# Sixteen pieces of dense work in an attention loop: one at a time in two of three steps, not two at a time in every third

## The reference

```python
def trunk_layer(x, cond, p, layer_idx, ctx):
    mod = jax.nn.silu(cond) @ p['w_ada'] + p['b_ada']            # six shifts, scales, gates
    sh1, sc1, g1, sh2, sc2, g2 = split(mod, 6)
    h = rmsnorm(x, p['g_pre_mix']) * (1 + sc1) + sh1
    y, new_ctx = token_mixer(h, p, layer_idx, ctx)
    x = x + g1 * rmsnorm(y, p['g_post_mix'])
    h = rmsnorm(x, p['g_pre_ffn']) * (1 + sc2) + sh2
    x = x + g2 * rmsnorm(expert_choice_ffn(h, ...), p['g_post_ffn'])

def token_mixer(h, p, layer_idx, ctx):
    q, k, v, z, xbc, dt_raw, g = split(h @ p['w_in'])
    ...
    g_attn, g_ssd = split(sigmoid(g), 2)
    merged = g_attn * (o_attn @ p['w_o_attn']) + g_ssd * (o_ssd @ p['w_o_ssd'])
    return merged @ p['w_out'], new_ctx

def diff_attention(q, k, v, lam, lam_init, w_subln):             # per block of 128 queries, 8 heads
    s = einsum('bqhmd,bkhmd->bhmqk', q, k) * scale               # two score maps per head
    pr = softmax(s)
    a = pr[:, :, 0] - lam * pr[:, :, 1]
    o = einsum('bhqk,bkhe->bqhe', a, v)
    return rmsnorm(o, w_subln) * (1.0 - lam_init)
```

## Time and profile before

| | us |
|---|---|
| median of 3 runs | 1917.01 (1915.61 to 1917.22) |
| the profiled execution | 1913.68 |
| its span, first to last instruction | 1911.9 |
| up to the attention stage | 634.0 |
| attention stage (634.0 to 800.3) | 166.3 |
| projections and routing (800.3 to 954.0) | 153.7 |
| experts (954.0 to the end) | 957.9 |

### The profile page before, as it was taken

The page is one execution under the profiler, slowest core; times in us unless marked ns, Lnnn a source line. Parts: engine busy times, 40 slices in busy tenths (PEclk is TensorE's granted clock), DMA queues, the critical chain, the costliest instruction groups (busy, mean ns, idle before and its releaser), DMA issues.

```text
span 1911.9 us, 22583 instructions
## 1 busy us (share of the span) xinstructions
PE 1587.8 (83%) x9263; PEld 934.3 (49%) x9263; DVE 521.7 (27%) x1450; ACT 257.8 (13%) x607; POOL 90.2 (5%) x118
## 2 busy tenths in 40 slices
PE   6998888989999876798798777977779777787775
PEld 4654544545565443455464444544435444454442
DVE  2439779750021245524600001000010000100002
ACT  1323222210010112102100000000001000100001
POOL 0002212210000000100000000000000000000000
PEclk9998998989999888898799999999999999999998
DMA  7233333312323114644099999999999999999993
GB/s 321 89 135 121 110 132 110 143 45 88 110 101 129 56 44 191 239 175 178 0 380 426 426 428 426 426 427 428 427 422 427 427 428 427 421 428 427 427 427 156
DMA packets 40305, 512.92 MB, mean 268 GB/s; under 512 B 4608, under 2 KB 4736, under 8 KB 10384
## 3 DMA queue, kind: packets, MB, share of 16 engines
q1 hardware_dynamic: 33696, 488.32, 61.6%
q0 software_dynamic: 6368, 22.58, 3.2%
q10 hardware_dynamic: 144, 0.59, 0.1%
HBM read 506.65 MB, written 4.82 MB: 268 GB/s over the span
## 4 chain that ended last, share of the span: by engine, by line
PE 49%; DMA 34%; DVE 12%; issue 3%; ACT 1%; POOL 1%; SPq 0%; DVEq 0%; ACTq 0%
DMA arena<-in_expert_chunks 33%; PE psum L356 14%; PE psum L779 13%; PE psum L367 9%; PE psum L568 4%; DVE arena L1394 1%; PE psum L380 1%; DVE arena L1383 1%; PE psum L798 1%; DVE arena L1466 1%; PE psum L543 1%; PE psum L404 1%; PE psum L414 1%; PE psum L553 1%; PE psum L652 0%
## 5 line engine op out<-in xcount | busy, mean ns | idle before, releaser
L779 PE MATMUL psum<-arena 128*64 128x256 f32 x6144 | 708.3, 386 | 165.2 <-DMA arena<-in_expert_chunks 136.3
L779 PEld LDWEIGHTS psum<-arena 128*64 128x64 f32 x6144 | 432.5, 138 | 431.5 <-DMA arena<-in_expert_chunks 190.3
L356 PE MATMUL psum<-arena 128*128 128x384 f32 x1024 | 352.0, 503 | 11.0 <-ACT arena L1088 7.7
L356 PEld LDWEIGHTS psum<-arena 128*128 128x128 f32 x1024 | 200.8, 198 | 149.8 <-issue 21.2
L1665 DVE TENSOR_TENSOR arena<-arena,psum 128x256 f32<-128x256 f32 x64 | 26.9, 421 | 774.1 <-ACT arena L1143 774.1
L367 PE MATMUL psum<-arena 128*128 128x512 f32 x384 | 166.4, 592 | 1.8 <-DVE arena L1514 1.8
L367 PEld LDWEIGHTS psum<-arena 128*128 128x128 f32 x384 | 72.4, 190 | 90.2 <-issue 87.5
L1143 ACT ACTIVATE arena<-psum 128x256 f32<-128x256 f32 x64 | 24.6, 384 | 616.0 <-PE psum L779 616.0
L568 PE MATMUL psum<-arena 128*128 128x384 f32 x256 | 84.8, 494 | 1.8 <-DVE arena L1355 1.2
L1150 ACT ACTIVATE arena<-psum 32x256 f32<-32x256 f32 x128 | 48.0, 375 | 272.8 <-PE psum L779 271.7
L856 POOL TENSOR_TENSOR arena<-arena 128x1 f32<-128x1 f32 x45 | 25.8, 575 | 1200.4 <-DVE arena L1539 941.4
(11 more groups left out here) (236 smaller groups left out, 990.5 us busy)
## 6 DMA issues: line engine op xcount, KB each, us to landing
arena<-in_expert_chunks SPq DMA_DIRECT2D x192, 2048.0 KB, 25.5
arena<-in_mixer_chunks SPq DMA_DIRECT2D x40, 2048.0 KB, 8.0
arena<-cs_rows POOLq DMA_DIRECT2D x24, 512.0 KB, 5.7
arena<-in_h_cm POOLq DMA_DIRECT2D x8, 256.0 KB, 3.0
out_state<-arena POOLq DMA_DIRECT2D x8, 256.0 KB, 3.4
arena<-in_x_cm SPq DMA_DIRECT2D x1, 1536.0 KB, 8.7
arena<-in_x_sample POOLq DMA_DIRECT2D x1, 1024.0 KB, 5.8
out_xs<-arena POOLq DMA_DIRECT2D x2, 512.0 KB, 2.9
```

Source lines behind the costliest of these rows:

```text
L356: mm = pe.matmul(b[:, 0:NTOK], w[:, k, ct * P:(ct + 1) * P], src[:, k, :], start=k == 0, stop=k == KT - 1)
L779: mm = pe.matmul(psum[HALF * q:HALF * (q + 1), bank, 0:2 * P], src[:, k0 + k, :], w[:, k, 2 * P * q:2 * P * (q + 1)], start=bool(first and ...
```

## The change

The list of steps with dense work is written anew. There are still sixteen pieces in the same order. Before, steps 2, 5, 8, ..., 23 had two each; now steps 1, 2, 4, 5, 7, 8, ..., 22, 23 have one each, so the steps of the latent tiles have one and those of the context tile none.

```diff
-        beside_attn = {2 + 3 * n: p for n, p in enumerate(
-            [[("ga", 2 * n), ("ga", 2 * n + 1)] for n in range(4)] + [[("ada", 2 * n), ("ada", 2 * n + 1)] for n in range(2, 6)])}
+        attn_pieces = [("ga", n) for n in range(KT)] + [("ada", n) for n in range(4, 12)]
+        beside_attn = {1 + 3 * m // 2: [p] for m, p in enumerate(attn_pieces)}
```

## The result

The changed kernel is slower: 1932.5 us median of 6 runs (1930.1 to 1943.2) against 1916.4 of 6 runs before; ratio 1.0093, 95% interval 1.0067 to 1.0119, which is +13 to +23 us. The forecast was 1918.5, and 1909 to 1929 its range.

What follows compares the result with a forecast made beforehand. No engine is full in attention, whose chain of hand-overs passes each us to the end; the experts are a DMA weight stream. +7.1 us at full clock less 5.6 from the clock gave +1.5, so 1918.5 us, range 1909 to 1929.

Steps and rivals of the forecast that it cites:

- The frame: Attention's gains or losses reach the end unchanged, DMA costs nothing, POOL's queue holds nothing new; context step 0.40 us shorter.
- The full-clock sum: Attention steps with TensorE at full clock: -0.4 gate part, -2.7 and +5.85 modulation, +4.4 last pair, total +7.1 us.
- 0.322 each and 5.15 a piece: Time on PE at full clock of one record and of a 16-record gate piece, in us.
- 1.71 a piece: Time on PE at full clock of one modulation piece, in us, from a last pair of 3.42.
- X+1.90: PE's first piece in a latent step starts 1.90 us after X, the moment DVE begins the step's row maximum.
- the last pair's cover: Pair 23 was wholly hidden under DVE; splitting it loses that cover, sum +4.4 us in the last steps.
- The clock term: Dense pieces at low clock: pairs lose 16.0 us today, single pieces would lose 10.4, so 5.6 us less.
- Small work at the low level I take as equal in both: PE's small work beside the pieces in attention was taken to lose equally in both kernels, so no difference.
- the choice of nothing for first pieces: Pieces in first latent steps lose nothing to low clock, since some 1.6 us of idle precedes them.
- The prices of 1.2 and 1.7 for second pieces: Low-clock loss in second latent steps: 1.2 us for each of three gate pieces, 1.7 for each of four modulation pieces.
- Rival 2: Most attention pieces, first ones too, run at low clock: 26.6 us lost, +18 in all, 1935 us; chance 0.13.
- rival 3: Score map, transposes and value product around second modulation pieces also run at low clock: +5 us, 1922; chance 0.17.

Runs made afterwards that it cites:

- second profile: The changed kernel run once more without any edit, to get another profile: 1931.6 us, with attention 175.8 us against 186.2 in its first profile.
- before_filler: Kernel before, plus products nothing reads: two before score maps of context and second latent steps, three before the pair; ratio to the kernel before 0.9974.
- ga_alone: Kernel before with only the eight gate pieces split to one per step, modulation pieces kept in pairs; ratio to the kernel before 0.9999.
- after_filler: Changed kernel, plus two or three products nothing reads in steps 3 to 23 where PE was expected to wait; ratio to the kernel before 1.0007.
- last_pair: Changed kernel with modulation pieces 10 and 11 together again in step 23, the other fourteen one at a time; ratio to the kernel before 1.0032.

## Why the forecast was wrong

Step lengths in us, from one row maximum to the next (the last line: from that of step 23 to DVE's last copy of the loop), worked out from the starts in each timeline:

| step | before | changed, first profile | second profile | with filler | forecast at full clock |
|---|---|---|---|---|---|
| 10, gate, first latent | 3.37 | 10.99 | 9.18 | 9.18 | 8.95 |
| 11, gate, second latent | 15.81 | 12.46 | 10.87 | 9.59 | 9.23 |
| 12, context | 4.22 | 3.87 | 3.87 | 3.86 | 3.82 |
| 13, modulation, first latent | 3.37 | 7.63 | 5.92 | 5.92 | 5.51 |
| 14, modulation, second latent | 9.92 | 9.69 | 9.74 | 7.27 | 6.75 |
| 15, context | 5.26 | 5.19 | 5.14 | 4.41 | 4.36 |
| 22, first latent | 3.38 | 5.92 | 5.92 | 5.92 | 5.51 |
| 23 to the end | 12.98 | 18.23 | 18.03 | 16.03 | 15.2 |

**The frame held.** Attention passes its time on to the end unchanged (1111.0 against 1111.6 us behind it), DMA and POOL played no part, the context step got shorter by 0.35 (forecast 0.40), waits appeared where they were placed, and with filler the step lengths are those of the forecast to within about 0.5 us (the last line of the table apart).

**The full-clock sum was too low: +7.1 forecast, about +11.3.** Full clock in the kernel before is worked out from its steps where it was at full level, or from `before_filler` (a second latent step with a gate pair 14.15) and `ga_alone` (with a modulation pair 7.42): 164.2 less 8.1 for gate pairs, 5.6 for modulation pairs and 0.6 for step 21 leaves 149.9, against 161.2 in `after_filler`. (The profile of `before_filler` bears this out: 149.9 + 3.0 + 4.5 for what is said of it above is its 157.4.) The mis-sized term is "0.322 each and 5.15 a piece" and "1.71 a piece". These came from the spacing of records inside a long block; a block standing alone also has its end, 5.40 and 1.92 us; the 0.2 that are left in a first latent modulation step lie half before the piece (X+2.00, not X+1.90) and half behind it. Sixteen blocks have eight more ends than eight pairs, 1.8 us of the 4.2 that were missing; the 0.2 are another 0.8, and the rest is spread over the loop in amounts too small to name a cause. It shows in each first latent modulation step (5.92, not 5.51), and in the last pair's cover: 5.6 us, not 4.4.

**The clock term had the wrong sign: 5.6 less loss forecast, 0.3 more measured, or 10.7 more.** The low level costs the kernel before 14.3 us (164.2 - 149.9; 16.0 forecast), the changed one 14.6 in its second profile (175.8 - 161.2) and 25.0 in its first, where 10.4 was forecast. Two sentences failed. "Small work at the low level I take as equal in both": beside each second modulation piece score map, transposes and value product now run low as well, 4.4 us in the second profile against 0.6 in the kernel before (second latent steps, context steps and the last line of the table against those with filler, less the pieces). And the choice of nothing for first pieces, "shorter than the 2.50 us in front of the pair at 711.07, so nothing": they lost nothing in the second profile, and 0.7 to 1.8 us each in five of eight cases of the first. The length of the pause just ahead does not decide it: in steps 10 and 13 PE stood idle for 2.04 and 2.13 us ahead of the piece in the second profile, where the clock was full, and for 1.18 and 1.27 us in the first, where it was low. The prices of 1.2 and 1.7 for second pieces were right in the second profile; in the first, three second gate pieces lost 1.7 to 2.8. The mistake was to price a level that differs from one execution of the same program to the next as if the program fixed it. Rival 2 named this mechanism and asked too much of every piece; rival 3 was right about small work.

**Together.** +11.3 at full clock and +0.3 or +10.7 from the level give the two profiles, +11.6 and +22.0 in attention; the timed runs, +16 and +18 by medians and by ratio, lie between. The two kernels with filler lie only 6 us apart, 3.8 in attention and 2.2 in the experts. That this is near the forecast's 7.1 is chance: the kernel before is 7.5 us above its full clock there, as worked out above.

**The Trainium skill** (TensorE: Matmul & The Clock Gate, section "Loop structure matters more than you think") says that matmuls back to back stay warm and that a long wait between them, there for a DMA, lets PE go cold. The trace agrees in direction: with a wait ahead of each group the granted clock is 0.50 to 0.80 in seven of the eleven single pieces shown from the changed kernel's two profiles. The order in the step decides as much here: the same list behind the products, with the modulation transposes last, has 0.99.

**What stays open** is how often each pattern occurs, and what sets it. Up to step 12 six kernels of this study have the same attention program on every engine, and in their seven profiles the gate part took 86.2, 86.2, 87.7, 88.7, 95.1, 95.2 and 95.3 us. Ten runs of one kernel spread over 19 us (`last_pair`), where 25 runs of the kernel before lie within 9. The gate half alone measured 0.9999; in its one profile attention took 160.8 us against 164.2, and with an interval of 3 us to either side the two agree.

## What to carry to other kernels

Work that fills an engine's gaps should stand behind what its partners wait for in the same step, not before it; that order was worth 24 us here, and the same cut of the work was worth -12 us behind it and +16 without it. Before splitting a block, price the wait ahead of it and its own end once for each part, and look for the part that was free: the last pair lay wholly under DVE. Where a level of the clock is in play, one profile is one draw: take more than one, and add filler work to both kernels to see what the level costs, looking in each profile whether the filler itself stands in the way.

## What the runs showed that I had not expected

- Ahead of the experts' loop nothing but 97 records of filler was added, and the experts took 960.1 and 962.3 us against 957.4 to 957.8 in every other profile, that with filler in steps 12 to 23 alone (56 records) among them at 957.6. In the view of waits from 960 us on, PE's waits for nothing shown ("issue") at the expert products rose from 16.5 us in 3 waits to 22.6 and 23.5 in 6, in pieces of up to 5.8 us. What it waits for there was not tried.
- The rounds of three steps with single gate pieces repeat themselves, in a short or a long form, for one and the same program: steps 7 to 9 and 10 to 12 took 24.0 and 23.9 us in the second profile of the changed kernel (9.24 + 10.90 + 3.87, 9.18 + 10.87 + 3.87) and 25.6 and 27.3 in its first (9.24 + 12.47 + 3.86, 10.99 + 12.46 + 3.87).
